# Linear attention on one Trainium2 core: the gates' logarithm ahead of the convolution, the bias tables read and masked earlier

## The reference, cut to what matters

```python
p = x @ w_in                                     # 3592 columns
ya = dilated_attention(aq, ak, av, rel_bias)     # 8 heads of 64, bias by distance, dilated mask
bq, bk = silu(causal_conv(...)) ; bv             # 4 heads of 128, convolution over 4 tokens
bi, bf = gates + gate_b                          # input and forget gate of each token and head
yb = sigmoid(bo) * head_norm(mlstm(bq, bk, bv, bi, bf))
y  = concatenate([ya, yb]) @ w_out
h  = layer_norm(ALPHA * x + y)
```

## Time and profile before

| what | value |
|---|---|
| median of three runs without a profile | 2640.08 us (2638.53 to 2644.58) |
| the profiled execution | 2621.77 us, of which the span is 2620.0 us |
| busy in the span | PE 2473.7 us (94%), DVE 1715.6 (65%), ACT 1082.8 (41%), POOL 81.5 (3%) |
| mean granted clock of PE | 0.975 of full speed |
| main memory | 496.33 MB read, 191 GB/s over the span |
| the mixer `ab` | from about 1436 to 1623 us of the span |

### The profile page before, as it was taken

One profiled execution on the slowest core, in us unless ns is written; L12 is line 12 of the kernel. 1 busy time (PEld: TensorE's weight loads), 2 busy tenths in 40 slices (PEclk: granted clock), 3 DMA queues, 4 the chain that ended last, 5 costly groups with the idle time before them and its releaser, 6 DMA issues.

```text
span 2620.0 us, 37877 instructions
## 1 busy us (share of the span) xinstructions
PE 2473.7 (94%) x16006; PEld 2189.7 (84%) x16006; DVE 1715.6 (65%) x2325; ACT 1082.8 (41%) x1295; POOL 81.5 (3%) x116
## 2 busy tenths in 40 slices
PE   3999989999999998999999989999999988999998
PEld 3999759999998878997999878788887857788886
DVE  6887576877887265544656564557996365647895
ACT  2333264334332032222334352546774252546773
POOL 0000000000000004430000000000000000000000
PEclk9999989999999999999999888999999989999999
DMA  6886305774774330001644620747994410747991
GB/s 289 329 320 244 121 25 197 291 276 177 292 287 188 129 113 1 1 1 67 252 180 146 180 71 10 296 189 301 373 349 177 167 66 1 291 175 306 368 369 49
DMA packets 48272, 501.91 MB, mean 192 GB/s; under 512 B 4968, under 2 KB 9448, under 8 KB 10856
## 3 DMA queue, kind: packets, MB, share of 16 engines
q1 hardware_dynamic: 42480, 490.52, 49.4%
q10 hardware_dynamic: 5624, 8.97, 1.4%
HBM read 496.33 MB, written 3.15 MB: 191 GB/s over the span
## 4 chain that ended last, share of the span: by engine, by line
PE 83%; DVE 10%; DMA 3%; ACT 2%; issue 2%; POOL 1%; ACTq 0%; SPq 0%; DVEq 0%; POOLq 0%
PE PS L565 25%; PE PS L1190 25%; PE PS L635 7%; PE PS L611 4%; PE PS L528 2%; PE PS L940 2%; PE PS L927 2%; DMA ring<-stream 2%; PE PS L936 1%; PE PS L648 1%; PE PS L1284 1%; PE PS L548 1%; DVE work L1829 1%; DMA xT<-x_in 1%; POOL work L2629 1%
## 5 line engine op out<-in xcount | busy, mean ns | idle before, releaser
L565 PE MATMUL PS<-x_part_hi,w_up_hi 128*128 128x256 f32 x1408 | 403.7, 287 | 11.9 <-DVE x_part_lo L1900 6.5
L565 PE MATMUL PS<-x_part_hi,w_up_lo 128*128 128x256 f32 x1408 | 398.2, 283 | 0.0
L565 PE MATMUL PS<-x_part_lo,w_up_hi 128*128 128x256 f32 x1408 | 398.2, 283 | 0.0
L2429 DVE TENSOR_TENSOR ring_low<-ring,m_w_up 128x2048 fp32r<-128x2048 f32 x128 | 293.1, 2291 | 130.9 <-ACT m_w_up L1677 130.9
L1677 ACT ACTIVATE m_w_up<-ring 128x2048 fp32r<-128x2048 f32 x128 | 245.3, 1917 | 184.2 <-PE PS L1190 183.8
L565 PEld LDWEIGHTS PS<-x_part_hi,w_up_hi 128*128 128x128 f32 x1408 | 269.8, 192 | 15.5 <-issue 8.0
L565 PEld LDWEIGHTS PS<-x_part_lo,w_up_hi 128*128 128x128 f32 x1408 | 270.0, 192 | 0.0
L565 PEld LDWEIGHTS PS<-x_part_hi,w_up_lo 128*128 128x128 f32 x1408 | 269.8, 192 | 0.0
L1190 PE MATMUL PS<-m_w_up,xg_hi 128*128 128x512 f32 x640 | 251.7, 393 | 3.8 <-DVE work L2443 3.8
L1190 PE MATMUL PS<-ring_low,xg_hi 128*128 128x512 f32 x640 | 252.8, 395 | 0.0
L1190 PE MATMUL PS<-m_w_up,xg_lo 128*128 128x512 f32 x640 | 252.1, 394 | 0.0
(11 more groups left out here) (516 smaller groups left out, 5186.6 us busy)
## 6 DMA issues: line engine op xcount, KB each, us to landing
ring<-stream SPq DMA_DIRECT2D x133, 2048.0 KB, 7.8
ring<-stream SPq DMA_DIRECT2D x88, 1536.0 KB, 6.6
work<-stream SPq DMA_DIRECT2D x48, 1024.0 KB, 8.5
hT<-stream SPq DMA_DIRECT2D x16, 1024.0 KB, 7.3
ring<-stream SPq DMA_DIRECT2D x3, 1152.0 KB, 5.6
const<-const_tables ACTq DMA_DIRECT2D x1, 2336.5 KB, 18.5
bias_scratch<-work ACTq DMA_DIRECT2D x1, 2048.0 KB
work<-bias_scratch ACTq DMA_DIRECT2D x2, 1024.0 KB, 7.8
```

Of the source, the lines that this page charges most:

```text
L565: last = mm(out, w[a][:, lo:lo + P], x[b][:, at:at + T], start=start and i == 0, stop=stop and i == 2, skip_group_check=skip)
L2429: tt_(ring_low[n][:, part], ring[n][:, part], m_w_up[g % 3][:, :].bitcast(F32), ALU.subtract).then_inc(S("up_split"), 1)
```

## The change

On DVE the two steps of the gates' logarithm move ahead: from behind the convolution's first half to right behind the low half of step 4, and the low half of step 5 and the convolution follow them. On ACT the wait for the table's write and the two reads (`load_bias`) move from behind the copy of piece 1 to behind the high halves of steps 10 and 11, ahead of the copy of piece 0. On DVE the wait for the tables, the addition of the mask and the low half of step 14 move from behind the chain of the numerators to ahead of it, behind the denominators' sums; the low half of step 15 moves into the attention, behind its step 2. No instruction is added or removed.

```diff
--- before.py
+++ after.py
@@ -1634,6 +1634,8 @@
                 fn(ls(100, 4), ls(100, 4), ACT.Exp).then_inc(S("lexp_ready"), 1)
                 copied(6, W(A_BO, 1024), 0, ACT.Sigmoid)
                 mix_highs("ab", 10, 11)
+                act.wait_ge(S("bias_stored"), 16)
+                load_bias(A_BM)
                 copied(0, W(A_Q, 1024), 6)
                 mix_highs("ab", 12)
                 line.next("lturned")
@@ -1643,8 +1645,6 @@
                 fn(ls(104, 4), bank(3, 4, 16), ACT.Copy).then_inc(S("state_copied"), 1)
                 mix_highs("ab", 13)
                 copied(1, W(A_K, 1024), 0)
-                act.wait_ge(S("bias_stored"), 16)
-                load_bias(A_BM)
                 mix_highs("ab", 14)
                 line.next("lnum_ready")
                 fn(ls(4352, 1024), flat(4, 2), ACT.Copy).then_inc(S("lnum_copied"), 1)
@@ -2295,15 +2295,16 @@
                             else:
                                 last = stt(qk[:, i, :], raw[:, i, j:j + T], w, qk[:, i, :], ALU.mult, ALU.add)
                         done(last, "conv_ready" if j == 3 and hi == 8 else None)
-                dve.wait_ge(S("ab_copied"), 1)
-                mix_lows("ab", 4, 5)
-                conv(0, 4)
+                mix_lows("ab", 4)
                 line.next("softlog_ready")
                 g = ls(0, 16).rearrange("p (t g) -> p t g", t=2)
                 sl = ls(160, 16).rearrange("p (t g) -> p t g", t=2)
                 lf = ls(16, 8).rearrange("p (t h) -> p t h", t=2)
                 done(ts_(lf, g[:, :, 4:8], 0.0, None, ALU.min))
                 done(tt_(lf, lf, sl[:, :, 4:8], ALU.subtract), "lin_fed")
+                mix_lows("ab", 5)
+                dve.wait_ge(S("ab_copied"), 1)
+                conv(0, 4)
                 line.next("cumsum_ready")
                 b, bl, gi = ls(24, 8), ls(32, 8), ls(40, 8)
                 v.tensor_copy(b, bank(7, 8))
@@ -2352,6 +2353,10 @@
                 den = ls(88, 8)
                 done(v.tensor_reduce(den, tiles(ss, P), AX.X, ALU.add))
                 hh = ls(4352, 1024)
+                dve.wait_ge(S("bias_in"), 32)
+                bm = W(A_BM, 8 * ATT).rearrange("p (h c) -> p h c", c=ATT)
+                done(tt_(bm, bm, C("dilated").unsqueeze(1).broadcast_to([P, 8, ATT]), ALU.add))
+                mix_lows("ab", 14)
                 line.next("lnum_copied")
                 line.next("linter_ready")
                 done(ts_(sc, sc, P ** -0.5, None, ALU.mult))
@@ -2392,11 +2397,7 @@
                     line.next("x_rounded")
                     hi, low = (part[:, 1024:2048] for part in mix_y["ab"])
                     tt_(low, ls(4352, 1024), hi.bitcast(F32), ALU.subtract).then_inc(S("mix_ready"), 1)
-                mix_lows("ab", 14, 15)
-                dve.wait_ge(S("bias_in"), 32)
-                bm = W(A_BM, 8 * ATT).rearrange("p (h c) -> p h c", c=ATT)
-                done(tt_(bm, bm, C("dilated").unsqueeze(1).broadcast_to([P, 8, ATT]), ALU.add))
-                attention("ab", {4: [linear_out], 5: [lambda: mix_lows("ab", 16)], 6: [linear_low]})
+                attention("ab", {4: [linear_out], 5: [lambda: mix_lows("ab", 16)], 6: [linear_low], 2: [lambda: mix_lows("ab", 15)]})
                 mix_lows("ab", 17)
                 layer_norm("ab", 0, by_half("ab"))
```

## The result

The changed kernel takes 2617.75 us, the median of five runs (2611.22 to 2626.53); the kernel before, timed beside it, 2638.53 us (2634.06 to 2644.58). The ratio, estimated from all ten runs, is 0.9931, with a 95% interval of 0.9903 to 0.9959 (the two medians alone give 0.9921): shorter by 0.41% to 0.97%, which is clear of the scatter and well under 2%. The forecast was 2625.9 us with a range of 2622 to 2634.

What follows compares the result with a forecast made beforehand. TensorE (PE), busy 83% of the span, was taken as the bound, so only its idle or low-clock stretches could be won. 8.1 + 6.1 = 14.2 us off 2640.08 gave 2625.9 us, range 2622 to 2634.

Steps and rivals of the forecast that it cites:

- The step that failed: Whole kernel: 14.2 us taken off the unprofiled median of 2640.08 gives 2625.9 us; three-run medians move about 2 us.
- The saving itself: Mixer stage: 8.1 us from the first part plus 6.1 from the second, 14.2 us in all.
- a measurement tells 0.2% from no change: Whole kernel: a difference of about 0.2% (5.3 us) can be told from no change.
- First part: Gates' logarithm ahead of DVE's convolution: saves PE's 5.4 us wait, 2.3 of clock and 0.4 in the cumulative sum, 8.1 us.
- The choice of the clock: Fifth piece on PE: clock stays up without the idle stretch, full 2.33 us taken, 0 as other end.
- The first rival: Fifth piece: small matmuls keep the clock low, only 11.5 us saved, 2628.6 us; chance 0.10.
- What is late next: Sixth piece after the first part: DVE's low half of step 6 has 2.6 us to spare, PE does not wait.
- the fourth rival: Waits only move, to the stabiliser's maxima or a later copy; under 5.3 us left, some 2637 us; chance 0.08.
- The stabiliser's chain: DVE's maxima for the stabiliser, the least trusted slack after the first part; ends 0 and perhaps 1 us.
- Second part: Bias tables, mask and low halves before the attention: 7.8 − 0.7 − 1.0 = 6.1 us saved.
- the third rival: Tables land late, holding DVE's chain and the attention: 8.8 us gain, 2631.3 us; chance slower 0.03, mere delay 0.04.
- The load that took 22.3 us: Load issued at 1455.14 beside the table's write; the third rival's evidence that the reads might land 5.4 us late.

Runs made afterwards that it cites:

- the later sets: Kernel before, unedited, timed again beside the changed kernel and its versions; medians of 2633.14, 2636.34 and 2633.59 us.
- 8.3 alone: Kernel before with only the gates' logarithm moved ahead of the convolution; stage 134.83 us, ratio 0.9981.
- the filling matmuls: Kernel before plus unused matmuls while PE waits for the logarithm; with 10, stage 140.23 us; with 22, 145.04 us, ratio 0.9996.
- 6.4 alone: Kernel before with only the reads, mask and low halves 14 and 15 moved; stage 136.78 us, ratio 0.9989.
- the last version: Changed kernel with low halves 15 and 16 moved behind the attention; stage 126.08 and 121.51 us, ratios 0.9920 and 0.9934 against the kernel before.

## Why the prediction was wrong, point by point

**The step that failed** is the last one, from the saving to the time and its range: the starting level of 2640.08 us, a median of three runs, and with it "the median of three runs moves by about 2 us". The saving itself, 14.2 us, was right: the stage shows 14.5 to 15.7. The level was the median of three runs of a kernel whose single runs spread over 25.5 us. In the later sets, with 35, 26 and 19 runs, the kernel before had medians of 2633.14, 2636.34 and 2633.59 us. Three runs drawn again and again from the 35 give medians from 2628 to 2640 us in 95% of the draws (an estimate of mine from the set's single runs), so such a median moves by 6 us, not by 2, and 2640.08 lay at the upper edge. Its own runs had hinted at it: the profiled execution was 18.3 us faster, and I carried this over as a constant of profiling where it was one execution against three; in the later sets the profiled execution is once the slowest of its kernel's runs (2647.91 us) and once the fastest (2613.79).

The miss of 8.1 us comes apart like this, by the medians of all 85 and 29 runs: 5.3 us are the level (2640.08 against 2634.79), 0.5 us a larger saving (14.7 against 14.2), and 2.4 us that the changed kernel's first five runs came out low (2617.75 against 2620.12), which is scatter. With the later levels and the same 14.2 us the forecast would have been 2619 to 2622 us; 2621.06 and 2618.39 were measured. The sentence that a measurement tells 0.2% from no change was too hopeful as well: the interval of the ratio reached 0.28% to either side.

**First part.** Forecast 8.1 us, measured 8.3 alone. PE's wait is gone (5.4); piece 5 is 2.35 us shorter, forecast 2.33; the cumulative sum gave about 0.5, forecast 0.4. The choice of the clock, between 0 and 2.33, was right, and the filling matmuls show its cause. The first rival, a low clock in piece 5, did not occur in any of the profiles with the logarithm ahead (11.34 to 11.36 us in each).

**What is late next.** Both low halves of piece 6 were done at 1484.9 and piece 6 started at 1486.70, 1.8 us later; from 1485 to 1540.4 PE was busy for all of its 55.4 us, so the fourth rival, waits that only move, did not occur there. The stabiliser's chain, whose slack I trusted least, shifted with the rest.

**Second part.** Forecast 6.1 us, measured 6.4 alone. In that version the first maximum came 6.7 us sooner (forecast 7.1) and the attention took 0.4 us more (forecast 1.0), so two small misses partly cancel. With both parts the first maximum was expected 15.2 us sooner (8.1 + 7.8 − 0.7) and came 15.4 to 15.5 sooner. L2362 starts behind low half 14 as computed, and the part that ACT's square gives back is seen in DVE's wait of 1.20 us ahead of L2384, which was 1.73. Low half 15 was forecast at 1.0 us net; the changed kernel's attention took 0.3 us less to 1.1 us more than the two of the kernel before, so the runs neither show that price nor refute it. What I had not seen is the clock: I read the attention as DVE's, while with the clock at 0.54 PE is busy for 27.1 of its 28.8 us, and the clock there differs between executions.

**The transfers.** Landed in 7.6 us, nearly 12 us before DVE came to them (issue at 1506.1, addition at 1525.49). ACT issued them 2.7 us sooner than forecast, counted from the mixer's start: the issue (1506.09) lies ahead of the high halves of steps 10 and 11 (1507.18 and 1508.98), which stand before it in ACT's program, and not under the second of them. The load of the first output piece, which I had beside the reads, shared only their last 2 us. Late reads cost us for us, as the third rival had it. The load that took 22.3 us beside the table's write is to be held against the median of all ring loads of this size in the kernel before, the last number here:

```profile
ring<-stream SPq DMA_DIRECT2D x133, 2048.0 KB, 7.8
```

The Trainium skill, page "DMA: Bandwidth & Descriptors", section "Issuing engines are not separate DMA queues", says that transfers started by different engines run on the same 16 DMA engines; the 22.3 us beside the write that ACT had issued agree with this. The reads in the kernel after are no test of it, for the same 2 us.

**Later stages** keep their length on the whole, but not in one execution: they moved by 17 us between two profiles of the same program. The profile after has a longer span than the one before for this reason (4.5 us ahead of the mixer, 14.5 behind it), and not by a loss of the change.

What stays open: why the clock comes back sooner in some executions than in others, in the gates, in the attention and in the stages behind it. The program is the same; no run here tells. Open is also what low half 15 costs inside the attention, beyond that it is less than the differences between executions.

## What to carry to other kernels

In this case two short results were worth 14.5 to 15.7 us of a stage of 143. A short result that another engine waits for belongs ahead of the long work in its engine's queue, at the place where its own inputs are ready: the idle time ahead of the next waiting instruction is free (here 5.8 us were left of it). Price such an edit in the stage, between two marks on the bound engine: here the kernel before repeated to 0.01 us, where whole executions spread by 1%. But take more than one profile where the clock changes inside the stage, as the changed kernel's three lay 1.2 us apart and the last version's two 4.6; and take the level of the whole from many runs before putting a range around it. When PE's idle time went, the piece behind it got faster as well, so add the clock's share where the row behind the idle stretch shows a low clock; and before taking work from an engine's queue, see which engine is busy at the clock that is granted there.

## What the runs showed of the hardware

The granted clock of one program on one core was 0.962 to 0.975 over the span by execution, with the same instructions; the time followed it: the spans at these two clocks were 2646.1 and 2620.0 us, and over the 35 runs of the kernel before 0.001 less of the clock went with 1.65 us more (an estimate, a straight line through the single runs; 1.72 and 1.64 in the other two sets). Matmuls with 8 columns, busy for 5.5 us without a gap, were followed by the lower level (0.56 in the stretch behind them), whereas two pairs of them behind full matmuls, 0.5 us, left it at the upper. In one profile, the second of the last version, the clock came back sooner, and the way to piece 5 was 1.6 us shorter. Its window over the matmuls 18.9 to 22.1 us behind the mixer's start, and the same stretch in the changed kernel's third profile:

```profile
1462.40:1465.60 3.20, 3.20 (x29) 3.20 (x29) 0.34 (x2) 0.70 (x2) 0.00 (x0) 1.00 1.00 275
```

```profile
1462.00:1465.20 3.20, 3.20 (x17) 3.20 (x16) 0.34 (x2) 0.81 (x2) 0.00 (x0) 0.51 1.03 286
```

In the attention a higher clock by itself bought nothing in the kernel before's form of it (0.54 and 0.63, both 28.8 us), at most 1.2 us in the changed kernel's (28.49 us at 0.70, 29.68 and 28.82 at 0.60 and 0.59), and 3 us once two low halves had left DVE's queue (0.68 and 0.79, 27.09 and 24.11 us).
